# Second projection of the last feed forward: six of its eight groups by seven products of quarters, with weight sums and result sums made by transfers that add

## The reference

```
f = rmsnorm(h, pre_ff_g[l]) @ w_ff1[l]            # 512 x 1024 by 1024 x 4096
f = jnp.square(jax.nn.relu(f)) @ w_ff2[l]         # 512 x 4096 by 4096 x 1024
h = h + rmsnorm(f, post_ff_g[l])
```

## Time and profile before

| | |
|---|---|
| median of 3 runs | 1729.72 us (1729.71 to 1730.04) |
| profiled execution | 1730.73 us, its span 1729.0 us |
| PE busy, share of the span | 1715.3 us, 99% |
| DVE, ACT, POOL busy | 1209.1, 820.2, 46.4 us |
| second projection interleaved with pairs | about 1430 to 1698 us of the span |
| PE, DVE, ACT busy in six stretches of 40 us from 1440 | 40.0, 28.0, 15.4 us of 40 |

### The profile page before, as it was taken

How to read it: one execution, slowest core, us unless ns; L and a number is a source line. 1 busy time by engine, 2 the same in 40 slices (tenths; PEclk the granted TensorE clock), 3 DMA queues, 4 the chain that set the end, 5 groups by cost and what they waited for, 6 DMA issues and landing times.

```text
span 1729.0 us, 26320 instructions
## 1 busy us (share of the span) xinstructions
PE 1715.3 (99%) x10458; PEld 1497.2 (87%) x10458; DVE 1209.1 (70%) x1975; ACT 820.2 (47%) x1449; POOL 46.4 (3%) x103
## 2 busy tenths in 40 slices
PE   9999999999999999999999999999999999999998
PEld 8777788999999887777989999989888898999997
DVE  4588787777787735666877777868446876677776
ACT  4477744444445235664444444443565555333342
POOL 0212000000000000000000000000000000000000
PEclk9999999999999999999999999999999999999999
DMA  8343332333334232224133333352314224333331
GB/s 276 113 134 118 119 89 87 109 98 110 101 99 153 86 105 84 81 91 122 39 103 98 110 110 97 99 165 82 110 44 140 63 73 126 106 98 98 100 109 49
DMA packets 220125, 181.36 MB, mean 105 GB/s; under 512 B 9906, under 2 KB 178771, under 8 KB 220003
## 3 DMA queue, kind: packets, MB, share of 16 engines
q1 hardware_dynamic: 217954, 175.48, 33.1%
q0 software_dynamic: 2048, 4.20, 0.9%
HBM read 173.32 MB, written 7.38 MB: 105 GB/s over the span
## 4 chain that ended last, share of the span: by engine, by line
PE 93%; DVE 4%; ACT 1%; DMA 1%; issue 1%; POOL 0%; DVEq 0%; POOLq 0%
PE ps L733 29%; PE ps L734 28%; PE ps L735 28%; PE ps L1092 1%; PE ps L1137 1%; PE ps L1163 1%; PE ps L1112 1%; PE ps L1151 1%; DMA arena<-arena 1%; PE ps L987 1%; DVE wlo L1701 0%; DVE xl L1793 0%; PE ps L1102 0%; PE ps L972 0%; ACT whi L1321 0%
## 5 line engine op out<-in xcount | busy, mean ns | idle before, releaser
L1701 DVE TENSOR_TENSOR wlo<-raw,whi 128x1024 fp32r<-128x1024 f32 (+1 forms) x276 | 317.6, 1167 | 181.3 <-ACT whi L1321 181.0
L733 PE MATMUL ps<-xh,whi 128*128 128x256 f32 (+1 forms) x1016 | 332.4, 327 | 2.3 <-DVE xl L1793 2.3
L735 PE MATMUL ps<-xh,wlo 128*128 128x256 f32 (+1 forms) x1016 | 326.1, 321 | 0.0
L734 PE MATMUL ps<-xl,whi 128*128 128x256 f32 (+1 forms) x1016 | 325.9, 321 | 0.0
L1321 ACT ACTIVATE whi<-raw 128x1024 fp32r<-128x1024 f32 (+1 forms) x276 | 274.6, 1007 | 80.9 <-DMA raw<-in_w_ff 36.4
L733 PE MATMUL ps<-whi,hh 128*128 128x512 f32 x728 | 288.7, 397 | 1.4 <-DVE wlo L1701 1.3
L734 PE MATMUL ps<-wlo,hh 128*128 128x512 f32 x728 | 285.2, 392 | 0.0
L735 PE MATMUL ps<-whi,hl 128*128 128x512 f32 x728 | 283.6, 390 | 0.0
L733 PEld LDWEIGHTS ps<-xh,whi 128*128 128x128 f32 x1016 | 194.1, 191 | 25.8 <-issue 8.8
L735 PEld LDWEIGHTS ps<-xh,wlo 128*128 128x128 f32 x1016 | 194.1, 191 | 14.4
L734 PEld LDWEIGHTS ps<-xl,whi 128*128 128x128 f32 x1016 | 194.4, 191 | 12.2
(11 more groups left out here) (272 smaller groups left out, 2935.3 us busy)
## 6 DMA issues: line engine op xcount, KB each, us to landing
raw<-in_ffn_w_in SPq DMA_DIRECT2D x88, 512.0 KB, 3.8
raw<-in_w_ff SPq DMA_DIRECT2D x64, 512.0 KB, 4.2
raw<-in_ffn_w_out SPq DMA_DIRECT2D x44, 512.0 KB, 3.9
raw<-in_a_w_qkv SPq DMA_DIRECT2D x22, 512.0 KB, 5.5
raw<-in_w_in SPq DMA_DIRECT2D x20, 512.0 KB, 3.8
raw<-in_kv_w SPq DMA_DIRECT2D x16, 512.0 KB, 4.1
bias_skewed<-bias_rows SPq DMA_DIRECT2D x8, 640.0 KB
arena<-arena POOLq DMA_DIRECT2D x64, 64.0 KB, 2.7
```

The costliest lines, as they stand in the source:

```text
L733: e.matmul(o, ah, bh, start=start, stop=False, **more)
L734: e.matmul(o, ah, bl, start=False, stop=False, **more)
L735: return e.matmul(o, al, bh, start=False, stop=stop, **more)
L1701: e.tensor_tensor(lo[:, 0:n], src, f32(hi[:, 0:n]), ALU.subtract).then_inc(s.lo, 1)
```

## The change

Groups 1 to 6 of the second projection are now made by seven products of quarters each. A quarter product has 256 tokens, 256 hidden features and 512 columns: two pieces (`t` = 0, 1) of six matmuls of 512 columns. So a group has 14 pieces in place of 16, and the table has 2, 2, 1, 2.

- **Right operands (weights).** Seven splits of 128 x 1024 for each group in place of four. They lie in the four 512 KB buffers of x. Four plain loads for each group go through SP; four transfers for each group are issued by GpSimd and *add* a tile of `w_ff2` from HBM to what lies in the buffer. Three of these form a chain in one buffer (called a here): split, add, split, add, split, add, split. The split that needs a sum waits for its transfer (`s_a_sum`, `s_d_sum`).
- **Left operands (hidden).** The raw squared hidden lies in the space of `hh`; DVE makes four sums for each group (`left_sum`), and seven left operands are split (`left`, ACT L1518 and a DVE subtraction) into `hl`.
- **Results.** The products are added up in two chains of two banks each. After each piece ACT copies the bank, with its sign, to one of four buffers `evicted` (L1525), and a transfer of 256 KB issued by GpSimd adds that buffer to its tile of `mb` (L2404): 14 for each group. DVE adds nothing to `mb` in these groups. The next product of a chain waits for the copy (`s_evicted`), the copy waits for the transfer that used its buffer four pieces ago (`s_added`), and a transfer waits for the one before it to the same tile.
- **x parked.** At the start of the feed forward SP stores x to HBM (`park`), and loads it back behind the last split of group 6 (`unpark`). The gain vector of the last norm is loaded later, to another place.
- Several semaphores are merged; this moves no instruction.

```diff
-FEED_PIECES = ["1111"] + ["2222"] * 13
+FEED_PIECES = ["1111"] + ["2212"] * 13
+SEVEN_FIRST, SEVEN_LAST = 1, 6
+SEVEN = [("a11", 0, True, 0, 0, 1), ("a12", 1, True, 0, 0, 1), ("s1", 1, True, 1, 1, -1), ("s4", 1, False, 0, 1, -1),
+         ("s2", 0, False, 0, 1, -1), ("s3", 0, False, 1, 1, -1), ("a22", 0, False, 1, 0, 1)]
...
+            elif what == "seven":
+                p, = arg
+                b, c = p.bank, slice(p.t * 128, p.t * 128 + 128)
...
+                w.wait_ge(s.lo, p.unit + 1)
+                w.wait_ge(s.left_lo, p.u + 1)
+                if p.before is None:
+                    w.wait_ge(*freed[b])
+                else:
+                    w.wait_ge(s.evicted, p.before + 1)
+                for k in (0, 1):
+                    m = mm3(e, ps[b][:], lh[:, k, c], ll[:, k, c], wh[:, k, :], wl[:, k, :], p.start and k == 0, k == 1,
+                            skip_group_check=True)
...
+            elif what == "seven_post":
+                p, = arg
+                w.wait_ge(s.rows, p.value)
+                if p.sent >= 4:
+                    w.wait_ge(s.added[p.sent % 4], 16 * (p.sent // 4))
+                e.activation(self.evicted[p.sent % 4], ps[p.bank][:].rearrange("p (k c) -> p k c", k=2), ACT.Copy,
+                             scale=float(p.sign)).then_inc(s.evicted, 1)
...
+                for buffer, chain, source in right.sums:
+                    if chain == "a":
+                        w.wait_ge(s.lo, m + 1)
+                    else:
+                        w.wait_ge(s.right[buffer], right.before)
+                    e.dma_start(self.x[:, buffer, :].rearrange("p (k c) -> p k c", k=2), self.row_tile(*source),
+                                accum_op=ALU.add).then_inc(s.right_sum[chain], 16)
...
+                if p.earlier is not None:
+                    w.wait_ge(s.added[p.earlier % 4], 16 * (p.earlier // 4 + 1))
+                e.dma_start(self.mb[:, p.tile, p.nh * 512:p.nh * 512 + 512].rearrange("p (k c) -> p k c", k=2),
+                            self.evicted[p.sent % 4], accum_op=ALU.add).then_inc(s.added[p.sent % 4], 16)
```

More of the change, by code:

```diff
@@ L61, in __init__ @@
         self.kind, self.nh, self.t, self.bank, self.i = kind, nh, t, bank, i
-        self.norm, self.group, self.value = norm, group, None
+        self.norm, self.group, self.value, self.added = norm, group, None, None
+class Piece:
+    def __init__(self, u, unit, t, bank, start, before, value, tile, nh, sign, sent, earlier):
+        self.u, self.unit, self.t, self.bank, self.start, self.before, self.value = u, unit, t, bank, start, before, value
+        self.tile, self.nh, self.sign, self.sent, self.earlier = tile, nh, sign, sent, earlier
+class Right:
+    def __init__(self, buffer, need, sums=(), load=None):
+        self.buffer, self.need, self.sums, self.load, self.before = buffer, need, sums, load, None
 class Pair:
-    def __init__(self, kind, n, table, columns, blocks):
+    def __init__(self, kind, n, table, columns, blocks, first=None):
         self.kind, self.table, self.columns, self.blocks = kind, table, columns, blocks
@@ L234, in post @@
         self.release(job.bank)
-        if job.kind in ("up", "relu"):
+        if job.kind == "relu" and job.arg[-1] >= 4:
+            self.raw_ready[job.arg[-1]] = "sq_relu", job.i + 1
+            self.step("post", job, None)
+        elif job.kind in ("up", "relu"):
             self.step("post", job, self.block(job.arg[-1] % 8))
@@ L339, in rows @@
             if last:
-                r.i = self.count(kind)
+                r.i, r.added = self.count(kind), self.added.get((t, nh))
             k = (row0 + k0) % 8
@@ L350, in rows @@
                 self.step("rows_post", r)
+                if kind == "f" and group == 0:
+                    self.plain_rows = r.value
             yield
@@ L942, in unsplit @@
             return self.raw[:, tile % RAW, :], 1024
+        if kind == "seven":
+            return self.x[:, tile.buffer, :], 1024
         if kind == "s2":
@@ L1314, in scalar @@
                     w.wait_ge(s.raw[tile % RAW], self.raw_at[tile])
+                elif kind == "seven":
+                    what, value = tile.need
+                    w.wait_ge(s.right[tile.buffer] if what == "load" else s.right_sum[what], value)
                 else:
@@ L1754, in vector @@
                 for i, k in enumerate(pair.blocks):
+                    if pair.kind == "relu":
+                        w.wait_ge(s.rows, self.plan.entry_free[3])
                     w.wait_ge(s.hh, pair.hidden[i] + 1)
@@ L2259, in sync @@
                 m, = arg
-                _, _, tile = self.plan.units[m]
+                kind, right, tile = self.plan.units[m]
+                if kind == "seven" and right.load is not None:
+                    w.wait_ge(s.hi, m + 1)
+                    w.wait_ge(s.lo, m + 1)
+                    rows_load(*right.load)
                 if tile is not None and tile + RAW < len(self.plan.tiles):
```

319 lines of the change are left out of this document (248 added, 71 removed).

## The result

The changed kernel takes 2017.24 us (median of 4 runs, 2015.70 to 2017.95) against 1729.88 for the kernel before, run beside it on the same chip (1729.71 to 1731.33). The ratio is 1.1658, with a 95% interval of 1.1638 to 1.1678: **287 us slower**, far outside the range of 1712 to 1765. The forecast was "faster", at 0.54.

The account below looks back on a forecast made before the run. PE was taken to bound the second projection. From 1730.73 us, minus 16.3 for removed matmuls, plus 1 for ACT and DVE and 3 for group 6, gave 1718.4 profiled, stated as 1717.5; forecast 1713 to 1724, 8-in-10 range 1712 to 1765.

Parts of the forecast that it names:

- POOL, for one group: Second projection: GpSimd's 18 issues take 9 to 71 us a group, 25 chosen, hidden beside PE's 39.1.
- Rival 2: GpSimd becomes the bound, slower: 1803 us at 3 us an issue, 1905 at 4.0; chance 0.16, including the mixture with rival 1.
- The DMA engines: Second projection: 30.6 of 39.1 us a group if adding costs what copying costs, 47.8 at double; factor 1.4 taken.
- rival 1: Groups 1 to 6: the DMA engines become the bound, slower, 1766 us if adding costs double; chance 0.24.
- Waits in the stage: Second projection: weight sums estimated to land in 6.5 us; landing up to some 10 us costs nothing.
- PE, DVE, ACT: Second projection, each group: PE 39.1 us with 72 matmuls fewer in all (16.3 us), DVE 32.4, ACT 29.5.
- Group 6: Last group of the stage: few products left to cover landing sums, so PE waits 3 us.
- x parked: Storing x to HBM and reloading it costs 0; 1 to 3 us if the last weight tiles come late.
- the end: After the stage: last matmul, last addition and norm stay as they are, 0 us.
- Rival 4: Second projection: removing 72 matmuls doesn't count; given no chance of its own.

Follow-up runs that it names:

- Experiment 2: Kernel of GpSimd transfers alone, series of copies and adding transfers issued back to back, with 16384 bytes of descriptor room in place of 1024: 121.8 us.
- experiment 3: Changed kernel with 2048 bytes of descriptor room in place of 1024, the triangular matrix moved to make place: 1758.5 us.
- experiment 9: Changed kernel with 2048 bytes of descriptor room, result sums made plain copies, weight sums still adding: 1744.9 us.
- experiment 4: Changed kernel with its 1024 bytes of descriptor room, all adding transfers made plain copies (sums left out of the result): 1724.8 us.
- experiment 1: Kernel of GpSimd transfers alone, series of copies and adding transfers issued back to back, with the 1024 bytes of descriptor room of both kernels: 172.0 us.
- experiment 13: Kernel of a group's transfers alone, in the changed kernel's order beside plain loads, 16384 bytes of room: 371.6 us; 44.9 us a group with all adding.
- experiment 8: Changed kernel with 2048 bytes of descriptor room, weight sums made plain copies, result sums still adding: 1727.1 us.

## Why the prediction was wrong, point by point

- **The step that failed** is *POOL, for one group*: "18 issues", priced by issue time alone, "Hidden; it decides from 39.1 / 18 = 2.2 us an issue". The issue was 1.22 us; the 1.4, a middle chosen between 0.5 and 4.0 without a row, came near it by luck. What was missing is that an issue may start only when its descriptors have room. With 1024 B that made 4.13 and 6.3 us between issues, 90.6 us a group, where even the upper bound was 71. The size stands in both kernels, outside the diff, and the prediction never looked at it: the 64 transfers of before moved 32 rows each, these move 256. Experiment 2 removes the wait by a change of the room alone, experiment 3 gives back 259 us.
- **Rival 2** had the place right ("its waits ... stand in one queue"), but neither the mechanism (POOL was busy for 9.7 of 40 us, not throughout) nor the price: its dearest case was "at 4.0, 71 us a group, 1905", its range ended at 1900, and 2017 was measured. It held 0.16, too little for a term whose bounds were 9 and 71 us a group.
- **The DMA engines.** The base came out: "30.6 of 39.1 us if adding costs what copying costs" against 30.2 to 30.4. That is in part luck, since it counts 256 packets of 1 KB for each result sum, and as copies these went in 64 of 4 KB (last section). The factor was "1.4, nearer to the copies that rows show"; it measured (44.9 - 13.4) / 17.2 = 1.83, and 1.90 with 2048 B. That is over the 1.5 up to which the engines stay ahead of PE and over the 1.65 of the tie with before. So with room for descriptors **rival 1** decides: 1713.4 + 6 x (46.1 - 39.1) = 1755, and experiment 3 gave 1758.5. It had "1766" at double. The Trainium skill's ratio of 1.93 (Collectives: The Full Stack, Part 3, "Why ReduceScatter is half of AllGather"), which the prediction set aside, is what the full mix agrees with: its 46.6 us a group against 46.1 and 44.9. The series alone in experiment 2 give 1.76 and 1.60. The prediction's other estimate from the same passage, 16 GB/s for each engine that adds, gave 35.9 a group and did not hold.
- **Waits in the stage.** "A landing up to some 10 us costs nothing" was wrong. With the engines at 0.83, weight sums that land in 6.9 us cost 44.0 - 39.8 = 4.2 us a group (experiment 9), in part by the lower clock that PE was granted as it stood more. The counting of slack went buffer by buffer; ACT waits in one order and hands the delay on to DVE's low parts. Which of the waits is the first of that chain was not tested. In experiment 3 it needs no part of its own, since the engines alone need 46.1.
- **PE, DVE, ACT.** 72 matmuls fewer; 39.8 a group in experiment 4 against 39.1; DVE 33.4 of 40 against "near 33"; ACT 27.3 against "near 30". These terms stood, to within 0.7 us a group, 4 in all.
- **Group 6**: 3 us forecast; in experiment 4 PE stands 5.5 us there. The copies of weights landed in 4.6 us, for which the counting ("about 1 us" at 4.2, "about 5.5" at 6.5) gives under 2: the term was nearly half too small, and its counting too mild.
- **x parked, the end: 0.** Nothing in the after profile speaks against it; it was not tested alone.
- **Rival 4** (no effect of the removal): experiment 4, 6 us faster than before with PE at 99%, bears out that it deserved nothing.

No version here with the right result is faster than the kernel before. With all sums by transfers the best is 1758.5, with half of the result sums on DVE 1752.9 (ratio 1.0136). Where the work was taken off the DMA engines it had to go to DVE, which is at 84% already, or to GpSimd, which slows DVE. A layout with 2 KB rows for the result sums, which let three go in flight in experiment 1, was not tried; the `evicted` buffers lie in 1 KB stretches of `xh`.

## What to carry to other kernels

A transfer queue has three prices: the issue, the room for what is in flight, and the work on the engines. An operation that no row of the profile shows needs all three, measured alone before a kernel leans on it; two small kernels of transfers show the 4.1 us (experiment 1) and the factor of 1.8 (experiment 13) here. And if bounds are as far apart as 9 and 71 us a group, the middle is no estimate: such a term deserves most of the doubt.

## What the runs showed of the hardware

- Descriptor room: with 1024 B one adding transfer of 256 rows is in flight; of 128 rows of 2 KB three are issued back to back, and three copies of 256 rows of 1 KB. Starts of the first kind are 4.1 us apart (6.1 from HBM) against 1.22 with 16384 B. The profile names the wait only "issue".
- For the same 38.81 MB GpSimd's queue shows 31424 packets when sums add and 12224 in experiment 4, where they copy: the copies go in fewer and larger packets. Alone (experiment 2) eight copies of 256 KB show 640 packets, 128 of them under 512 B, so 512 of 4 KB for 2.10 MB; eight sums show 2176, so 2048 of 1 KB. Whether that is why they cost less was not tested by itself.
- An adding issue takes 1.22 us, a copy of the same shape 0.72.
- `tensor_tensor` on GpSimd (1793 ns for 128x512) beside DVE's with two SBUF operands: 1222 to 1785 ns and 685 to 1064 ns on DVE in the mean, and 1.22 to 2.27 us for a split that overlaps one.
- The DMA share reaches 1.04 to 1.14 when the engines are full, and the kernel can still be unhindered at 1.11 (experiment 8): the share tells that engines are busy, not that somebody waits.
